# A latent attention that computes its output transposed, with the values as the stationary operand

## What is computed

```python
q = (cq @ w_uq).reshape(B, S, 8, 192)
k_nope, v = (ckv @ w_ukv) ...
s = einsum('bqhd,bkhd->bhqk', qi, k) * scale
s = where(key_pos <= q_pos, s, -1e30)
pr = softmax(s, axis=-1)
mo = einsum('bhqk,bkhv->bqhv', pr, v)
...
a_ret = (ro * silu(rg)) @ w_br
mixed = sigmoid(gr) * a_ret + sigmoid(gm) * (mo @ w_bm)
x = x + mixed @ w_o
```

## Time and profile before

| | |
|---|---|
| median of 3 runs | 1202.94 us (1200.70 to 1203.14) |
| profiled execution, its own time | 1204.8 us |
| its span | 1203.0 us |
| PE matmul busy | 1175.5 us, 98% |
| PE weight load busy | 969.0 us, 81% |
| DVE busy | 749.4 us, 62% |
| ACT busy | 629.1 us, 52% |
| GpSimd busy | 61.7 us, 5% |
| DMA | 203.4 MB, mean 169 GB/s |
| chain of work that ended last | PE 92%, DVE 2%, ACT 2%, DMA 1%, issue 1% |

### The profile page before, as it was taken

One profiled execution on the slowest core, in us unless ns is written; L12 is line 12 of the kernel. 1 busy time (PEld: TensorE's weight loads), 2 busy tenths in 40 slices (PEclk: granted clock), 3 DMA queues, 4 the chain that ended last, 5 costly groups with the idle time before them and its releaser, 6 DMA issues.

```text
span 1203.0 us, 15916 instructions
## 1 busy us (share of the span) xinstructions
PE 1175.5 (98%) x5735; PEld 969.0 (81%) x5738; DVE 749.4 (62%) x1004; ACT 629.1 (52%) x970; POOL 61.7 (5%) x76
## 2 busy tenths in 40 slices
PE   9999999999999999999989999998999999999997
PEld 6787888888878888888878887777888877888886
DVE  6877566465575756656568788444645666556564
ACT  6686554354467555444455555555744454444443
POOL 2001000000000100000030051000000000000000
PEclk9999999999899999999999999999999999999999
DMA  9544455555455555555466555433565645555542
GB/s 292 183 140 125 164 186 190 192 189 162 140 149 156 167 175 192 191 189 190 141 191 199 177 159 153 125 92 92 167 192 176 191 149 183 187 189 192 192 162 84
DMA packets 94754, 203.44 MB, mean 169 GB/s; under 512 B 7853, under 2 KB 10309, under 8 KB 94704
## 3 DMA queue, kind: packets, MB, share of 16 engines
q1 hardware_dynamic: 93216, 199.61, 52.1%
q0 software_dynamic: 1184, 3.04, 0.8%
q10 hardware_dynamic: 304, 0.14, 0.0%
HBM read 201.70 MB, written 1.06 MB: 169 GB/s over the span
## 4 chain that ended last, share of the span: by engine, by line
PE 92%; DVE 2%; ACT 2%; DMA 1%; issue 1%; POOL 0%; ACTq 0%
PE pair L705 17%; PE pair L707 17%; PE pair L706 17%; PE turn_ps L802 7%; PE pair L802 7%; PE turn_ps L804 4%; PE score L707 4%; PE score L705 4%; PE score L706 4%; PE pair L804 4%; PE turn_ps L733 3%; DVE w_lo L1652 1%; PE score L1094 1%; DMA raw<-in_w_in 1%; PE score L1093 0%
## 5 line engine op out<-in xcount | busy, mean ns | idle before, releaser
L1652 DVE TENSOR_TENSOR w_lo<-raw,w_hi 128x1024 fp32r<-128x1024 f32 (+2 forms) x381 | 458.1, 1225 | 190.0 <-ACT w_hi L1216 188.6
L1216 ACT ACTIVATE w_hi<-raw 128x1024 fp32r<-128x1024 f32 (+2 forms) x381 | 391.5, 1049 | 224.7 <-DMA raw<-in_mlp_w 64.0
L705 PE MATMUL pair<-w_hi,a_both 128*128 128x512 f32 (+3 forms) x560 | 226.3, 404 | 5.9 <-ACT lat_sb L1261 4.8
L707 PE MATMUL pair<-w_hi,a_both 128*128 128x512 f32 (+3 forms) x560 | 217.8, 389 | 0.0
L706 PE MATMUL pair<-w_lo,a_both 128*128 128x512 f32 (+3 forms) x560 | 217.0, 388 | 0.0
L802 PE MATMUL pair<-a_both,w_hi 128*128 128x512 f32 x384 | 143.3, 398 | 1.6 <-DVE up_sum L1698 1.6
L802 PE MATMUL turn_ps<-a_both,w_hi 128*128 128x512 f32 x384 | 142.6, 396 | 1.9 <-DVE p_lo L1668 1.9
L705 PEld LDWEIGHTS pair<-w_hi,a_both 128*128 128x128 f32 x560 | 108.0, 193 | 28.5 <-ACT lat_sb L1261 5.1
L707 PEld LDWEIGHTS pair<-w_hi,a_both 128*128 128x128 f32 x560 | 107.7, 192 | 21.6
L706 PEld LDWEIGHTS pair<-w_lo,a_both 128*128 128x128 f32 x560 | 108.0, 193 | 19.8 <-issue 1.2
L804 PE MATMUL turn_ps<-a_both,w_lo 128*128 128x256 f32 x384 | 107.5, 280 | 0.0
(11 more groups left out here) (363 smaller groups left out, 1635.0 us busy)
## 6 DMA issues: line engine op xcount, KB each, us to landing
raw<-in_mlp_w SPq DMA_DIRECT2D x128, 512.0 KB, 3.3
raw<-in_w_in SPq DMA_DIRECT2D x64, 512.0 KB, 3.6
raw<-in_w_up SPq DMA_DIRECT2D x32, 512.0 KB, 3.6
raw<-in_w_down SPq DMA_DIRECT2D x32, 512.0 KB, 3.2
raw<-in_attn_w_in SPq DMA_DIRECT2D x24, 512.0 KB, 5.5
raw<-in_mlstm_w_in SPq DMA_DIRECT2D x24, 512.0 KB, 3.8
raw<-in_w_br SPq DMA_DIRECT2D x16, 512.0 KB, 3.8
raw<-in_attn_w_out SPq DMA_DIRECT2D x8, 512.0 KB, 3.7
```

The source lines that it names most:

```text
L705: pe.matmul(o, hi, whi, start=start, stop=False)
L707: return pe.matmul(o, lo, whi, start=False, stop=stop)
L1216: act.activation(w_hi[:, k % RING, 0:n], raw[:, k % RING, 0:n], ACT.Copy).then_inc(hi_ready, 1)
L1652: dve.tensor_tensor(w_lo[:, k % RING, 0:n], raw[:, k % RING, 0:n], w_hi[:, k % RING, 0:n], ALU.subtract).then_inc(lo_ready, 1)
```

## The change

PE now makes the output of a head transposed: the values are the stationary operand and the transposed probabilities move, one product of 256 columns and one of 128. What comes out has the features in the partitions and the positions in the columns, which is how bm0 and bm1 need it. The reciprocals would then have to be applied along the columns; so DVE multiplies the probabilities by them before they are transposed, two instructions a head behind the reciprocal, and PE's transposes wait for these (`l_scaled`). The order of the three transposes changes so that the keys of the first block lie side by side. ACT empties a head with one instruction of 256 columns and no scale. The four turns of o in br0 are gone from all three engines; in their slots ACT makes `a_hi` and DVE `a_lo` from SBUF, 512 columns an instruction.

```diff
-            order.append((f"lv{h - 1}", 2, 0))
+            order.append((f"lv{h - 1}", 1, 0))
...
-    split("moT", pairs)
...
             def mla_probs(h):
-                pe.wait_ge(l_exped, h + 1)
-                transposed(f"lp{h}", [l_e[:, h % 2, j * P:(j + 1) * P] for j in range(3)])
+                pe.wait_ge(l_scaled, h + 1)
+                transposed(f"lp{h}", [l_e[:, h % 2, j * P:(j + 1) * P] for j in (2, 0, 1)])
...
             def mla_value(h):
...
-                pe.matmul(bank[:, 0:P], l_pt[:, h % 2, TALL], v[0], start=True, stop=True)
-                pe.matmul(bank[:, P:S], l_pt[:, h % 2, 0:P], v[0], start=True, stop=False)
-                pe.matmul(bank[:, P:S], l_pt[:, h % 2, P:S], v[1], start=False, stop=True).then_inc(turn_filled, 1)
+                pe.matmul(bank[:, 0:S], kv[:, 0, h, NOPE:], l_pt[:, h % 2, 0:S], start=True, stop=False)
+                pe.matmul(bank[:, P:S], kv[:, 1, h, NOPE:], l_pt[:, h % 2, S:SCORE], start=False, stop=True)\
+                    .then_inc(turn_filled, 1)
...
-            dense("br0", {2 * n + 1: (lambda n=n: mo_turn(2 * n)) for n in range(4)})
+            dense("br0")
...
-                act.wait_ge(l_reced, h + 1)
-                for tt in range(TT):
-                    act.activation(lo_sb[:, tt, h * P:(h + 1) * P], turn_bank(f"lv{h}")[:, tt * P:(tt + 1) * P],
-                                   ACT.Copy, scale=l_rec[:, h % 2, 1 - tt:2 - tt]).then_inc(turn_act, 1)
+                act.activation(lo_t[:, h, :], turn_bank(f"lv{h}")[:, 0:S], ACT.Copy).then_inc(turn_act, 1)
...
+            def split_mo(n):
+                wait_group(act, "gr1")
+                act.wait_ge(turn_act, turn["lv7"]["act_end"])
+                two = slice(2 * n, 2 * n + 2)
+                act.activation(a_hi[:, two, :], lo_t[:, two, :], ACT.Copy).then_inc(mo_hi, 1)
...
             def mla_recip(h):
                 dve.wait_ge(l_exped, h + 1)
-                if h >= 2:
-                    dve.wait_ge(turn_act, turn[f"lv{h - 2}"]["act_end"])
-                dve.reciprocal(l_rec[:, h % 2, :], l_sum[:, h % 2, :]).then_inc(l_reced, 1)
+                b = h % 2
+                dve.reciprocal(l_rec[:, b, :], l_sum[:, b, :]).then_inc(l_reced, 1)
+                dve.wait_ge(l_reced, h + 1)
+                for j, cols in enumerate((WIDE, TALL)):
+                    last = dve.tensor_scalar(l_e[:, b, cols], l_e[:, b, cols], l_rec[:, b, j:j + 1], None, ALU.mult)
+                last.then_inc(l_scaled, 1)
...
             def mix_ret(n):
...
+                dve.wait_ge(mo_lo, 4)
...
+            def split_mo(n):
+                dve.wait_ge(mo_hi, n + 1)
+                two = slice(2 * n, 2 * n + 2)
+                dve.tensor_tensor(a_lo[:, two, :], lo_t[:, two, :], a_hi[:, two, :], ALU.subtract).then_inc(mo_lo, 1)
```

More of the change, by code:

```diff
@@ L417, in build @@
         flat_q = lq_sb[:, :, :, :].rearrange("p t h d -> p (t h d)")
-        lo_sb = flat_q[:, 0:TT * D].rearrange("p (t n) -> p t n", t=TT)
-        mix = lo_sb
+        lo_t = flat_q[:, 0:TT * D].rearrange("p (h s) -> p h s", s=S)
+        mix = flat_q[:, 0:TT * D].rearrange("p (t n) -> p t n", t=TT)
         KV = TT * MLA_H * (NOPE + P)
@@ L540, in build @@
         l_exped = sem("l_exped")
+        l_scaled = sem("l_scaled")
+        mo_hi = sem("mo_hi")
+        mo_lo = sem("mo_lo")
         l_reced = sem("l_reced")
@@ L599, in build @@
                  "lat": (lat_hi, lat_lo, "q_lat_norm_2", 0), "roT": (b_hi, b_lo, "ret_norm_2", 0),
-                 "moT": (a_hi, a_lo, None, 0), "mixT": (b_hi, b_lo, None, 0), "pT": (p_hi, p_lo, None, 0)}
+                 "mixT": (b_hi, b_lo, None, 0), "pT": (p_hi, p_lo, None, 0)}
         def split_parts(name):
@@ L709, in wait_source @@
             def wait_source(source, c):
+                if source == "moT":
+                    pe.wait_ge(mo_lo, c // 2 + 1)
+                    return
                 name, j = turn_of(source, c)
@@ L1103, in mla_value @@
                 pe.wait_ge(turn_act, turn[f"lp{h}"]["act_end"])
-                v = [kv[:, tt, h, NOPE:] for tt in range(TT)]
-                pe.matmul(bank[:, 0:P], l_pt[:, h % 2, TALL], v[0], start=True, stop=True)
-                pe.matmul(bank[:, P:S], l_pt[:, h % 2, 0:P], v[0], start=True, stop=False)
-                pe.matmul(bank[:, P:S], l_pt[:, h % 2, P:S], v[1], start=False, stop=True).then_inc(turn_filled, 1)
+                pe.matmul(bank[:, 0:S], kv[:, 0, h, NOPE:], l_pt[:, h % 2, 0:S], start=True, stop=False)
+                pe.matmul(bank[:, P:S], kv[:, 1, h, NOPE:], l_pt[:, h % 2, S:SCORE], start=False, stop=True)\
+                    .then_inc(turn_filled, 1)
             def mla_slot(n):
@@ L1160, in _ @@
             dense("gr1")
-            def mo_turn(c):
-                pe.wait_ge(turn_act, turn["lv7"]["act_end"])
-                transposed(f"moT.{c}", chunks_of(lo_sb, c, 2))
-            dense("br0", {2 * n + 1: (lambda n=n: mo_turn(2 * n)) for n in range(4)})
+            dense("br0")
             dense("br1")
@@ L1608, in _ @@
             empty("gr1", [gr[:, tt, HALF:D] for tt in range(TT)], ACT.Sigmoid, row_norm(5))
-            dense("br0", {2 * n + 1: (lambda n=n: split_turn(f"moT.{2 * n}")) for n in range(4)})
+            def split_mo(n):
[3 more added lines that the diff above has]
+                act.activation(a_hi[:, two, :], lo_t[:, two, :], ACT.Copy).then_inc(mo_hi, 1)
+            dense("br0", {2 * n + 1: (lambda n=n: split_mo(n)) for n in range(4)})
             dense("br1")
```

## The result

| | before | after |
|---|---|---|
| median | 1202.34 us (4 runs, 1200.70 to 1203.14) | 1214.04 us (4 runs, 1212.89 to 1215.89) |
| profiled execution, its span | 1204.8, 1203.0 us | 1214.36, 1212.6 us |
| PE matmul busy | 1175.5 us | 1176.1 us |
| PE granted clock, mean of the span | 0.992 | 0.989 |

The ratio is 1.0101, interval 1.0083 to 1.0118: the changed kernel is 11.7 us slower where 8.0 us had been forecast. On the base of the forecast, 1202.94 us, that is 1215.1 us, just above the range. The direction is as forecast, and so are the waits and their cause; what the sum lacks is the clock.

A forecast was written before the change was run, and what follows sets the result against it. The matrix engine, busy 98% of the span, was taken as the bound. Waits for the scaling, 9.77 us, less 1.80 us for br0's turns, gave 8.0 us over the median of 1202.94: 1210.9 us, range 1207.5 to 1214.3.

The forecast's parts named there:

- DVE's order decides: Latent attention slots: reciprocal and scaling stand behind mask and maxima, so PE's transposes wait; 9.77 us more in all.
- The pair at 0.54 us from the first attention: DVE's two scaling multiplications per head, 256 and 128 wide, taken at the time of a like pair in the trace: 0.54 us.
- Part 2 at nothing: Latent attention values as stationary operand: at best 0.26 us a slot, covered by the new wait in slots 2 to 8; nothing taken.
- Part 3 at -1.8 us: br0: four groups of transposes of o leave the matrix engine, 0.45 us each, 1.80 us less.
- The 0.14 us that slots 4 and 8 get back from ACT's lost eviction: Slots 4 and 8: ACT's copy of the transposes no longer queues behind evictions, so 0.77 us later becomes 0.63 each.
- the clock's term: Whole kernel: the new waits cost no clock in the sum; lower clock levels appeared only as a rival.
- One more drop, after slot 1 or 4: Latent attention: one further fall to half clock after a new wait, 1.5 us, giving 1212.4 us; chance 0.12.
- One of its own signs of being wrong: Matrix engine: the prediction is wrong if a wait under 2 us is followed by products 0.42 us apart.
- rival A: Latent attention: the waits also cost clock, 1212.4 us with one drop (0.12), 1221.4 us with one at seven slots (0.02).
- Many short waits: Matrix engine: the skill's rule that frequent short idle times swing the clock, held not borne out by the trace of before.
- the far rival: Latent attention: a clock drop after each of the seven slots, 10.5 us more, 1221.4 us; chance 0.02.

The follow-up runs named there:

- second measurement: The changed kernel timed once more, unchanged, against the kernel before: 1213.53 us, 1.0079.
- the scaling twice: The changed kernel with a second pair of multiplications, by one, behind the first: 1223.87 us, 1.0161 against the kernel before.
- the version with all orders: Changed kernel, DVE scaling ahead of mask and maxima, ACT's exponentials and DVE's scaling of heads 3 and 7 ahead of the gates: 1196.76 us, then 1196.93 us.
- scaling alone: The kernel before with only DVE's multiplications and the transposes waiting for them; output and turns of o as before: 1216.4 us, 1.0108.
- The filled waits: The changed kernel with products of zeros on PE ahead of the wait for the scaling: 1210.58 us, 1.0056 against the kernel before.

## Why the prediction was right in its waits and wrong in its clock

**DVE's order decides: right.** Six waits of 1.95 us once and 1.1 us five times, two of 1.68 and 3.76 us, all for the scaling, were forecast as 2.0, about 1.2 to 1.3, 1.7 and 3.8. In start times, which the working used, slots 1 to 4 are within 0.02 us of it. (In slot 2 the idle time shown, 1.10 us, is less than the delay of 1.26: the last product of the values ends at 793.98, and the transposes of before had started 0.15 us ahead of such an end.) Swapping the order takes 10.2 us back, 1.5 us of them a drop.

**The pair at 0.54 us from the first attention: right**, 0.55. Adding the two durations of the earlier trace rows would have been 0.08 us a slot too much.

**Part 2 at nothing: right.** The product took 0.76 us for 0.77; there was nothing for the wait to cover.

**Part 3 at -1.8 us: right in the trace**, by the landmarks around br0. In the timed runs it isn't resolved by itself.

**The 0.14 us that slots 4 and 8 get back from ACT's lost eviction: right in kind.** Without scaling the two waits shrank by 0.20 and 0.19 us; with it slot 4 came out at 0.65 for 0.63.

**The step that failed is the clock's term, which the sum had at nothing.** "One more drop, after slot 1 or 4" was priced at 1.5 us, and 1.5 us is what it cost, but it got a chance of 0.12 and so stood outside the number. It happened after slot 4 in both traces of the changed kernel, 1.58 us by the table, and a further one behind the wait near 1000 us in both, 1.3 us, of which the prediction says nothing. One of its own signs of being wrong came true with it: a wait under 2 us (1.68) followed by products 0.42 us apart. The evidence against rival A was thin: one wait of 1.94 us with no drop behind it, and one of 1.09 us. That was read as a rule ("the new waits of 1.3 us are shorter than the first of these") where the traces show no such rule. In the stage, and at the one wait near 1000 us (for DVE's `p_lo`), the traces hold 56 waits of 0.89 us or more. How many were followed by a drop, over all fourteen traces:

| wait of PE | where | drops / waits |
|---|---|---|
| 0.89 to 1.11 us | stage | 1 / 18 |
| 1.38 to 1.69 us | stage | 4 / 10 |
| 1.95 to 2.54 us | stage | 3 / 6 |
| 2.98 us and more | stage | 8 / 8 |
| 1.67 to 1.95 us | near 1000 us | 5 / 14 |

Elsewhere in the same traces PE waits 1.0 us near 750 us, 14 times in all and never followed by a drop, and 3.3 to 5.5 us near 625 us, with the lower level around its end all 14 times.

Read as chances (in hindsight, so this is a sizing and no test), the changed kernel's waits hold 5 x 1/18 = 0.3 drops for the five short ones, 0.4 for slot 4 and 0.5 for slot 1: about 1.2 more in the stage, 1.8 us, beside the one of slot 8 that both kernels have. The sum would have been 8.0 + 1.8 = 9.8 us, 1212.7 us. With the fourteen waits near 750 us the first row would be 1 / 32 and its share smaller still; what else than its length decides what follows a wait is not shown.

The timed runs bear out both halves, the waits and the missing term, as estimates. In the second measurement the kernels are 9.1 us apart by the means and their clock losses 1.6 us (11.1 and 9.6), which leaves 7.6 us for a forecast of 8.0 without the clock. In the first they are 12.1 us apart, and the clock loss is some 4 us above the 9.0 of the kernel before (from other sessions: of its own four runs only one has a clock on record, 0.992), which leaves about 8. With the scaling twice they are 19.4 and 6.9 us, leaving 12.5 for 8.0 + 4.6. So the 11.7 us of the first measurement are the waits as forecast, less br0, and a clock loss of up to 4 us, part of it outside the stage. The wait near 1000 us had a drop in both traces of the changed kernel and in neither of the kernel before, 1.3 us; but over all traces it was 5 of 9 without the turns of o and 0 of 5 with them, and the two traces of the version with all orders, one with and one without, show that it can be missing without them. Whether giving up the turns makes it more frequent stays open. The second measurement, 1.0079, is 9.5 us on the base of the forecast; the two intervals overlap.

**Many short waits.** The Trainium skill ("TensorE: Matmul & The Clock Gate", section "A second HAM failure mode: psum-queue depth-cycling") says that frequent short idle times between groups of matmuls let the clock go up and down. I had written that the trace of before doesn't bear it out. The traces of the changed kernel bear it out in part: with waits of 1.1 to 2.0 us every 7 us the clock fell once (changed kernel, both traces) or twice (scaling alone) a stage, and with those of 1.7 to 2.5 us four times, slot 8's long wait left out; it didn't fall at each of them, which was the 1221.4 us of the far rival. The filled waits show that it is the idle time and not the order of the work: the transposes wait for DVE as long, PE has products to do meanwhile, and there is no drop.

## What to carry to other kernels

When a step on one engine is made to wait for another engine's small work, read where that work stands in the other engine's program, not how long it is: the same sixteen multiplications lengthen the stage by 9.9 us behind mask and maxima, by 6.9 us behind a weight split that waited for a third engine (drops of the clock included both times), and by 0.1 us in front of both. Then price each new wait of the matrix engine twice, once as the wait and once as a chance of a slow restart, and let the second stand in the forecast as soon as there are several; one trace in which it didn't happen is one draw. Where two executions of one kernel differ by 3 us in a stretch that the change doesn't touch, judge a change of this size by the length of its own stage first.

## What the hardware showed that was not expected

- The same wait, 1.69 us between the same instructions, was followed by half the clock in slots 2 and 6 and by the full clock in slots 3, 5 and 7 of one execution. A drop came behind 1.09 us once and stayed away behind 2.30 us once.
- Behind slot 4's wait the transposes themselves were already slow (0.90 us for three in place of 0.55); in slot 2 of the kernel with the scaling twice they took 0.55 us and the slow products began only with the second. The fall needn't coincide with the end of the wait.
- The clock can fall while PE is busy: from 318 to 331 us, where it begins with products of 8 columns, it was busy throughout, at a granted clock of 0.61 in one execution and 0.87 in another. The last wait ahead of it, 0.96 us in the first, had ended 5 us before the fall. All fourteen traces have a fall there.
- A product of 256 and one of 128 moving columns in float32 took 0.76 us, three of 128 took 0.77 us.
